# A decoder-layer kernel: convolution, branches, mixing and retrieval run in two token passes

## What is computed

```
z   = x W_in                      q/k/v of 3 dilation groups | conv x_in, B, C | gate_a, gate_c
A   = dilated sliding-window attention (prompt, and samples against their caches)
Cv  = B * conv3(C * x_in)         causal depthwise convolution, width 3, over positions
mix = W_out[ sigmoid(gate_a) * (A W_pa) + sigmoid(gate_c) * (Cv W_pc) ]
h   = LN1(alpha x + mix);   y = LN2(alpha h + PEER(h))
PEER: 8 heads, product keys 128 x 128 -> 16384 single-neuron experts, the 16 best of each head
```

## Time and profile before

| | |
|---|---|
| three runs | 4303.24, 4302.79, 4301.15 us, median 4302.79 |
| profiled execution | span 4298.5 us (from first to last instruction); its own time is not listed beside it |
| engines busy | PE 3719.0, DVE 2907.8, POOL 1839.2, ACT 1132.3 us |
| moved by DMA | 982.88 MB |
| stages, us | prompt attention 727, sample attention 134, convolution 511, branches 159, mix 149, retrieval 440, gates 187, experts 1942, last norm 50 |

### The profile page before, as it was taken

One profiled execution on the slowest core, in us unless ns is written; L12 is line 12 of the kernel. 1 busy time (PEld: TensorE's weight loads), 2 busy tenths in 40 slices (PEclk: granted clock), 3 DMA queues, 4 the chain that ended last, 5 costly groups with the idle time before them and its releaser, 6 DMA issues. The chain is left out here.

```text
span 4298.5 us, 64136 instructions
## 1 busy us (share of the span) xinstructions
PE 3719.0 (87%) x24845; PEld 3504.5 (82%) x24845; DVE 2907.8 (68%) x5689; ACT 1132.3 (26%) x1847; POOL 1839.2 (43%) x1341
## 2 busy tenths in 40 slices
PE   8999997699998987974296899888999888899988
PEld 8899895499998965874286888888988888888886
DVE  3444433222222342999796999999999999999997
ACT  2323313111111011342394222222222222222221
POOL 0000000000000024576696777776676777777671
PEclk9999998799999998887598999999999999999999
DMA  4022122754444442100088999999999999999996
GB/s 147 20 75 64 28 72 88 290 202 168 159 163 141 144 140 70 31 23 1 20 232 289 392 371 369 376 379 376 365 369 373 373 385 367 373 377 373 374 357 228
DMA packets 441959, 982.88 MB, mean 229 GB/s; under 512 B 48893, under 2 KB 226429, under 8 KB 439778
## 3 DMA queue, kind: packets, MB, share of 16 engines
q0 software_dynamic: 153744, 561.32, 34.5%
q1 hardware_dynamic: 285570, 409.15, 27.3%
q10 hardware_dynamic: 2384, 8.91, 0.5%
HBM read 901.73 MB, written 131.28 MB: 240 GB/s over the span
## 5 line engine op out<-in xcount | busy, mean ns | idle before, releaser
L1918 POOL DMA_INDIRECT u_row<-in_peer_u_dram,eid x512 | 724.2, 1414 | 409.2 <-DVE dots L1977 305.8
L59 PE MATMUL e_ps<-coef_h,v_h 128*128 128x288 f32 x2048 | 642.8, 314 | 171.6 <-DVE v_l L1946 106.2
L1924 POOL DMA_INDIRECT v_row<-in_peer_v_dram,eid x512 | 617.6, 1206 | 191.5 <-issue 161.1
L1993 DVE SCALAR_TENSOR_TENSOR f_row<-v_row,g_coef,f_row 128x1024 f32<-128x1024 f32 x508 | 653.2, 1286 | 2.2 <-DMA v_row<-in_peer_v_dram,eid 2.0
L59 PE MATMUL e_ps<-hBh,u_h 128*128 128x288 f32 x2048 | 609.3, 298 | 49.3 <-DVE u_l L1939 49.1
L1977 DVE CUSTOM_DVE_ANT_0 u_row<-u_row,h_row 128x1024 f32<-128x1024 f32 x512 | 623.3, 1218 | 14.7 <-DMA u_row<-in_peer_u_dram,eid 14.6
L60 PE MATMUL e_ps<-coef_l,v_h 128*128 128x288 f32 x2048 | 626.4, 306 | 0.0
L61 PE MATMUL e_ps<-coef_h,v_l 128*128 128x288 f32 x2048 | 625.7, 306 | 0.0
L61 PE MATMUL e_ps<-hBh,u_l 128*128 128x288 f32 x2048 | 605.3, 296 | 0.0
L60 PE MATMUL e_ps<-hBl,u_h 128*128 128x288 f32 x2048 | 605.3, 296 | 0.0
L59 PEld LDWEIGHTS e_ps<-coef_h,v_h 128*128 128x128 f32 x2048 | 406.4, 198 | 207.0 <-DVE v_l L1946 133.4
(11 more groups left out here) (294 smaller groups left out, 7908.9 us busy)
## 6 DMA issues: line engine op xcount, KB each, us to landing
u_raw<-in_peer_uT_dram SPq DMA_DIRECT2D x128, 512.0 KB
v_raw<-in_peer_vQ_dram SPq DMA_DIRECT2D x256, 256.0 KB
s_g<-gate_block SPq DMA_DIRECT2D x9, 4096.0 KB, 16.1
x_gate<-s_g SPq DMA_DIRECT2D x64, 576.0 KB
out_o_kv_sample_dram<-in_cache_kv_w_dram SPq DMA_DIRECT2D x32, 1016.0 KB, 7.6
c_raw<-in_conv_tiles_dram SPq DMA_DIRECT2D x40, 512.0 KB, 3.5
w_raw<-in_w_in_dram SPq DMA_DIRECT2D x96, 192.0 KB
cache_v<-in_cache_vS_dram SPq DMA_DIRECT2D x8, 2304.0 KB
```

The costliest lines, as they stand in the source:

```text
L59: pe.matmul(out, lh, rh, start=first, stop=False)
L1918: pool.indirect_dma_start(urow[:, r % RING], None, io["peer_u"][0], bass.IndirectOffsetOnAxis(ap=eid[:, r:r + 1], axis=0)).then_inc(urow_i ...
L1924: pool.indirect_dma_start(vrow[:, r % RING], None, io["peer_v"][0], bass.IndirectOffsetOnAxis(ap=eid[:, r:r + 1], axis=0)).then_inc(vrow_i ...
L1993: dve.scalar_tensor_tensor(out=f, in0=vrow[:, r % RING], scalar=coef[:, s % 2, x:x + 1], in1=f, op0=ALU.mult, op1=ALU.add).then_inc(weighe ...
```

## The change

The stages from convolution to retrieval run twice, first for the 512 fetched tokens (`EARLY`, tiles 0 to 3, one chunk of 512), then for the other 576 (`LATE`, tiles 4 to 8, chunks of 288). The order is `prompt_attn`, `conv_gates`, `branches`, `mix_ln1`, `retrieve` of EARLY, clearing and barrier, `sample_attn`, the four of LATE, `build_gates`, `experts`, `ln2_out`. Each pass loads and splits all weights. The functions of the row steps now stand outside `experts` and every stage has places for them, but `ROWS_IN` gives these stages none.

Beside this:

- `conv_gates`: hardware loops written out; three weight buffers; three slots of PSUM; the split of the next unit crosses the end of a block; gates are stored by SP's queue; all cache copies are issued in the EARLY pass; two columns (`u_tail`) go over to LATE. LATE also loads `h_row` 0 and 1 and issues the first four u fetches.
- `branches`: loops written out; gate loads and merged stores on SP's queue.
- `mix_ln1`: 3 (EARLY) or 2 (LATE) weight buffers in place of 4; POOL no longer waits for the store of each tile.
- `retrieve`: the same per head, on 4 and on 5 tiles; the expert index `eid` is made at the end of EARLY.
- `experts`: no row steps ahead of the loop; 528 of them spread over the 512 slots, so that the last slot of each v phase has two; Gelu and the moves of `h_row` and `f_row` at the very slots that they belong to (dots of row 127, 255 done; rows 143, 271, 399, 527).

```diff
-CHUNKS = ((0, 384), (384, 384), (768, 320))
-HCHUNKS = ((0, TA), (TA, TB // 2), (TA + TB // 2, TB // 2))
+HB, TAIL, RING = 8, 2, 4
+NHB = GTILES * P // HB
+NROW = P * GTILES
+NSTEP = NROW + HB * TAIL
+ROWS_IN = (0, 0, 0)
...
+EARLY = Half("A", 0, GTILES, 0, TA, ((0, TA),), TA)
+LATE = Half("B", GTILES, NT - GTILES, TA, TB, ((0, TB // 2), (TB // 2, TB // 2)), SEQ - TA)
...
+def spread(y0, total, slots):
+
+    return [y0 + total * i // slots for i in range(slots + 1)]
...
-def conv_gates(nc, io, k):
+def conv_gates(nc, io, k, half, y0, rows):
...
+            for n in range(NQ):
+                store_gate(n)
+                load(n + 5)
+                if half is EARLY:
+                    for piece in PIECES[n % NU]:
+                        sp.dma_start(*cache_piece(*piece, n // NU)).then_inc(k["cache_moved"], 16)
...
+            split(0)
+            for n in range(NQ):
+                if n + 1 < NQ:
+                    split(n + 1)
...
+    at_row = spread(y0, NSTEP - y0, 2 * GE + (NGE - 1) * (2 * GE + NSL) + NSL)
...
+            def move_tiles(slot):
+
+                for y in range(at_row[slot], at_row[slot + 1]):
+                    t = (y - HB * TAIL) // P
+                    if y % P == P - 1 and y // P + 2 < GTILES:
+                        load_h_row(sp, k, io, y // P + 2)
+                    if y >= HB * TAIL and (y - HB * TAIL) % P == P - 1:
+                        store_f_row(sp, k, io, t)
...
             split_u(0)
             split_u(1)
-            for x in range(HB):
-                row(0, x)
             split_u(2)
             coefs(0)
-            for x in range(HB):
-                row(1, x)
             split_u(3)
...
+            phase(prompt_attn)
+            mixed(EARLY, (0, 0), (0, 0))
+        phase(mix_ln1, EARLY, 0, 0)
...
+            phase(retrieve, EARLY)
+
+        nc.clear_and_free_semaphores(nc.allocated_since(first_sems))
+        nc.all_engine_barrier()
+        c.enter_context(nc.sbuf_tensor("rows_place", [P, words], F32))
+        phase(sample_attn)
...
+        mixed(LATE, y0, counts)
+        phase(mix_ln1, LATE, y0[2], counts[2])
```

More of the change, by code:

```diff
@@ new lines, in row_step, with row_gelus @@
+def row_step(dve, k, y):
+    s, x = divmod(y, HB)
+    if s < NHB:
+        dot_row(dve, k, y)
+    if s >= TAIL:
+        weigh_row(dve, k, y - HB * TAIL)
+    if x == HB - 1 and 1 <= s <= NHB:
+        dve.wait_ge(k["row_gelu"], s)
+        dve.tensor_tensor(k["g_coef"][:, (s - 1) % 2], k["gelud"][:, (s - 1) % 2], k["gsel"][:, (s - 1) * HB:s * HB],
+                          ALU.mult).then_inc(k["row_coef"], 1)
+def row_gelus(act, k, y0, y1):
+    for y in range(y0, y1):
+        s, x = divmod(y, HB)
+        if x == HB - 1 and s < NHB:
+            act.wait_ge(k["dotted"], HB * (s + 1))
+            if s >= 2:
+                act.wait_ge(k["row_coef"], s - 1)
+            act.activation(k["gelud"][:, s % 2], k["dots"][:, s % 2], ACT.Gelu).then_inc(k["row_gelu"], 1)
@@ L828, in sem @@
         def sem(n):
[L829 to L836, removed]
+            return nc.alloc_semaphore(n + half.name)
@@ L875, in _ @@
+            for x in range(2):
+                sp.wait_ge(gate_out[x], 16 * KD)
         @block.gpsimd
         def _(pool):
[L877 to L884, removed]
+            if half is LATE:
+                for r in range(y0 + rows + RING):
+                    fetch_rows(pool, k, io, r)
@@ L1317, in _ @@
-            over_tiles(pool, step)
+            for i in range(TL):
+                x, n = i % 2, n_of(i)
+                at = (half.first + i) * P
+                N.affine(pool, i, x, n)
+                pool.wait_ge(N.ready, i + 1)
+                pool.dma_start(io["s_h"][at:at + n], N.y[:n, x]).then_inc(h_out[x], 16)
+                for r in range(at_row[i] + RING, at_row[i + 1] + RING):
+                    fetch_rows(pool, k, io, r)
+            for x in range(2):
+                pool.wait_ge(h_out[x], 16 * ((TL + 1 - x) // 2))
@@ L1523, in each @@
                 def each(f):
-                    for t in range(NT):
-                        f(t, rows_of(t))
+                    for t in range(TL):
+                        f(t, rows_of(half.first + t))
                     dve.drain()
@@ L1623, in build_gates @@
     NB = TB // GB
[L1624 to L1625 removed]
+    NTB = LATE.tiles
     NGR = GB // GT
@@ L1713, in _ @@
         def _(pe):
-            for y, t in enumerate(TILES):
-                n = rows_of(t)
+            for y in range(NTB):
+                n = rows_of(LATE.first + y)
                 if y >= 2:
@@ L2027, in _ @@
                                 add(g, m // 2 - 1)
-                        row(4 * g + 4 + m // HB, m % HB)
+                        rows(slot)
+                        slot += 1
                     add(g, KD - 1)
@@ L2031, in _ @@
                     e = GE * g + GE + 2 + j
-                    row(4 * g + 6 + j // 4, 2 * (j % 4))
+                    if g < NGE - 1:
+                        rows(slot)
                     if e <= KEYS:
@@ new lines, in mixed @@
+                    k[n] = conv.enter_context(nc.sbuf_tensor(n + half.name, [P, KD, half.n], F32R))
+                phase(conv_gates, half, y0[0], rows[0])
+                phase(branches, half, y0[1], rows[1])
+        first_sems = nc.snapshot_sems()
+        with ExitStack() as first:
+            for n in ("xAh", "xAl"):
+                k[n] = first.enter_context(nc.sbuf_tensor(n, [P, KD, TA], F32R))
+            phase(prompt_attn)
+            mixed(EARLY, (0, 0), (0, 0))
+        phase(mix_ln1, EARLY, 0, 0)
@@ L2248, in program @@
+        phase(experts, y0[3])
+        phase(ln2_out)
         with nc.Block() as block:
```

968 lines of the change are left out of this document (505 added, 463 removed).

## The result

The changed kernel takes 4441.77 us (median of 4 runs, 4437.11 to 4448.26) against 4301.97 for the kernel before: 1.0326 of its time, with a 95% interval of 1.0311 to 1.0341. It is slower by 140 us; 105 had been forecast (4407 us), with a range of 4370 to 4450. The profiled execution took 4442.81 us with a span of 4440.6.

A forecast was written before the change was run, and what follows sets the result against it. Products bound convolution and branches, nobody mix, DVE retrieval; PE and DVE are about level in experts. Convolution +1, branches +17, mix +43, retrieval +56, boundary +2, experts -15: +104 us, span 4402.5, plus 4.3 gives 4407 us; range 4370 to 4450.

The forecast's parts named there:

- Branches (+17): Branches: one more pass adds its start, end and slow clock, 15.5 us, plus 1.5 for copies still queued.
- faster: Rival, experts: early Gelus and moved SP waits shorten groups from 119 toward 101 us; 4150 us; chance 0.02.
- experts gains nothing because DMA sets its pace: Rival, experts: DMA at a share of 0.97 sets the pace, so no gain; 4422 us; chance 0.13.
- chain and copies together in part: Upper end of the range, 4450: retrieval's 4-tile chain and convolution's cache copies each cost part of their extra.
- term of 9 us for the copies: First convolution pass: weights queued behind cache copies sometimes come late; 9 us, bounds 0 and 25.
- bound by the copies: Rival, first convolution: copies and weights halve each other, backlog into branches, +20 to +30; 4430 us; chance 0.13.
- the ends scale: Retrieval: work behind the last marker, 69 us before, scales with tokens but for about 1 us of `eid`; +1.
- chain at half clock: Rival, early retrieval: PE's 14 us per head become 28 at half clock, above DVE's 23.8; 4440 us; chance 0.12.
- 12 of 15 are covered, the others cost 2.5 each, 7 us: Experts: doubled row-step slots mostly hide in DVE's wait for the next activation's Gelu; uncovered ones add 7 us.
- SP now waits in its stream for dots 127 and 255 and for the rows 143, 271 and 399 ...: 5 us: Experts: u and v loads stand behind SP's waits, with some 4 blocks' lead and share 0.97; 5 us.
- bound of +15: Experts, upper bound: nothing gained because DMA sets the pace, and each of SP's waits costs a buffer.
- DVE's wait for the store of `f_row` ... stays: Experts: DVE's wait for this store, 13.8 us in 3 places, was to remain unchanged.

## Why the prediction was right, and where not

- **Direction, size and bound.** Right: each stage pays its start, its end and what doesn't scale with the tokens twice, and this is nearly the whole of it. Branches (+17) and the steps of mix (13.4 and 13.3 us per tile) are on the number. The rivals *faster* and *experts gains nothing because DMA sets its pace* aren't what came: the head gained its 28 us, and three groups lost it again.
- **Luck in the number.** The forecast was 35 us too low. Mix, retrieval and experts all came out above it, 47 us together, and convolution 9 below; the median lies 1.2 us above the span and not 4.3. The range was drawn up to 4450 for "chain and copies together in part"; neither came, and 4441.77 lies in it for other reasons. Only the bounds of the single stages (mix +50, retrieval +80, experts +15) covered what happened where it happened.
- **Convolution.** The products took 220 and 258 us (222 and 254 forecast, with the slow clock behind each start), PE waited 2.6 us for `c_wl` in each pass. The term of 9 us for the copies was wrong: at a share of 0.92 and 336 GB/s they didn't hold PE up. The rival *bound by the copies* is out, and half the copies elsewhere gave the pass 2 us. They cost 4.5 us in branches, three times the 1.5 taken. (A single copy moves 0.5 to 2 MB, not the 4 MB that the prediction says.)
- **Mix.** +48.5 for +43: the fills were 35.6 and 41.7 us where 31 and 37 had been taken. Mis-sized, not misread: one buffer more takes 4.2 us off the first.
- **Retrieval.** +75 for +58. The step that was mis-sized is the part that doesn't scale: a pair of heads was to take 5.9 us more than a head before (52.4 - 46.5), 7.1 were measured (53.6 - 46.5), 49 us over seven heads and not 41. All of the difference is in the first pass, 25.2 us a head for 23.8; the second has 28.4 for 28.6. The step that failed is "the ends scale": they take 38.2 and 41.8 us for 69.3, 11 us more where 1 had been taken. DVE is busy for 52.0 us in them and was for 47.0, the rest is waiting in a chain of small instructions across POOL, ACT and DVE. The fills (+15 for +14) were right. The rival *chain at half clock* is out: DVE is busy for 160 of 176 us. POOL's share is now measured: 28 of 32 splits are worth 12.5 us, so by estimate the 16 that were added some 7.
- **Experts.** Head -28 (forecast -27): right. "12 of 15 are covered, the others cost 2.5 each, 7 us": nearly right, 0.4 us per plain group, some 5 in all, though two runs had first seemed to say the opposite. The step that failed in experts is "SP now waits in its stream for dots 127 and 255 and for the rows 143, 271 and 399 ...: 5 us": the groups with these rows have 35 us more. I had counted on a lead of 4 blocks; in a v phase the lead is four tiles of v and SP runs that far ahead, so it meets the wait early, stands there for 16.6 us, and the buffers run dry (8.5 us, twice). The bound of +15 had this in words ("each of SP's waits costs a buffer"), the sum did not. And "DVE's wait for the store of `f_row` ... stays" was true in length (12.4 for 13.8 us) and wrong in cost: it was beside DVE's wait for the Gelu before, and is in mid-phase now, where its group took 6 us more; that the place makes the difference is argued, not tested.

## What to carry to other kernels

Splitting a pass in two costs every stage its fill, its end and its per-head chain again; here that was 133 us on stages of 1260, and it has to be earned by something that the split makes possible. A wait put "at the very slot" into a queue that runs ahead holds up all that stands behind it; 16 us of waiting cost 8.5 us in the middle of a v phase, and 3 us at most where they fell at the end of a u phase. Put it where the data is long done. When work is spread evenly over slots, look where the period's edges fall, and compare groups one by one before explaining a sum: three long ones looked like fifteen small costs.

## What the runs showed of the hardware that was not expected

A store of 512 KB held its buffer for 9 us when it was issued from POOL's queue beside 512 KB row fetches on the same queue (27.0 us of waits in 3 places; median 9.0 us from issue to landing), and for 4 us from SP's (12.4 in 3 places; median 4.8). POOL's work slowed DVE's two-input instructions (673 and 270 ns for one of 128 x 64) and left MAX8 as it was (281 ns). And some 78 MB in 232.6 us, most of it copies from DRAM to DRAM, at a share of 0.92, left PE's products where they were: 220 us from first to last, 219 with half the copies.
